# First block on one core: token rows transposed before their norm is known, the norm applied to the projections instead

## The chip, the cores and the metric

The kernel runs on one core of a Trainium2 chip, as one program. The metric is the device time of that core in microseconds (us), from several runs of the same program; a smaller number is better. TensorE does the matrix products, ScalarE and VectorE do everything elementwise, GpSimd some small steps, and SyncE issues nearly all transfers from HBM.

## The reference, cut to what matters

Two transformer blocks over 256 tokens of width 1024. The part that the change touches is the start of the first block:

```
h = rms_norm(x, norm_mix)                 # x * rsqrt(mean(x*x) + eps) * gain
z = h @ w_in                              # (256, 2560)
zu, zv, zq, zk, zval = split(z)           # 512 columns each
u = gelu(zu);  v = gelu(zv)
a_out = u * (tril(W_s) @ layer_norm(v) + b)
o = differential_attention(q = zq / 8, k = zk, v = zval)
x = x + concat(a_out, norm(o)) @ w_out
x = x + memory_attention(rms_norm(x), rms_norm(mem), w_q_mem, w_kv_mem, w_o_mem)
x = x + mixture_of_32_experts(rms_norm(x))
```

A second block (attention and a squared-ReLU feed-forward of width 4096) and a last norm follow. All of it is fp32.

## The kernel before, in words

The 256 tokens are two halves of 128 rows (h = 0 and 1). A weight matrix is taken in units of 1 MB, each of which is split into a rounded high part, which ScalarE makes (`high(u)`, line 494, 128x2048), and a low part, the rest, which VectorE makes (`low(u)`, line 523, 128x2048). A product is then three matmuls, lines 433, 434 and 435 (`three`). The order of units in the first block is v.0, v.1, u0, u1, q0, k0, val.0, val.1, q1, k1, km0, km1, km2, out0 and so on. The first two are split in four pieces each (`rows_high`, line 891, and `rows_lows`, line 1112). Units share two sets of high and low tiles in turn, so `high(u)` of a unit waits until TensorE has ended the unit two places before.

The orders in which the engines work are written out by hand, one list per engine (`first_tensor`, `first_scalar`, `first_vector`, `first_sync`, `first_gpsimd`). Each engine takes its own list strictly in order and waits on semaphores of the others.

Before the change the rows of x are normed first. ScalarE squares and sums each half (`square_sum`, line 511), VectorE adds the epsilon (line 540), GpSimd takes the power -1/2 (line 548), and ScalarE and VectorE each scale half of the columns (lines 515 and 542). Then TensorE transposes the scaled rows (`turn`, line 484) into the PSUM banks hT00, hT01, hT10 and hT11 (half of the tokens, half of the features), and ScalarE and VectorE make the high part (`turned_highs`, line 505) and the low part (`turned_lows`, line 532) of the transposed rows, with the gain. The 256 rows of the memory go the same way later (memT); TensorE transposes them between the units u0 and u1.

Products leave their banks so: v.0 and v.1 (tokens in rows) through a Gelu on ScalarE; u0 and u1 (features in rows, tokens in columns) through a Gelu on ScalarE; q0, k0, q1 and k1 through a copy on ScalarE (`feature_out`, line 497); val.0 and val.1 through a copy on VectorE. The attention over pairs (head, half of the queries) goes by `diff_scores`, `diff_soft_a`, `diff_exp`, `diff_soft_b`, `diff_turn`, `diff_apply` for u = 0 to 7. `diff_scores(0)` waits for q0 and k0 to have left their banks, `diff_scores(4)` for q1 and k1. `gating` (lines 707 and 708) makes the product with W_s and adds the bias.

TensorE's list around the change, in short: transpose x; v.0; v.1; u0; transpose mem; u1; q0; transpose W_s; k0; diff_scores(0); val.0; diff_scores(1); gating; val.1; diff_scores(2); diff_turn(0); q1; diff_scores(3); diff_turn(1); diff_apply(0); k1; diff_scores(4); diff_turn(2); diff_apply(1); km0; and on.

Of the kernel before, what the change touches and what calls it, by code (L numbers as in the profile page):

```python
# [9 lines left out]
ALU = mybir.AluOpType  # L10
# [120 lines left out]
hT00 hT01 hT10 hT11 +v.0 +v.1 -v.0 -v.1 u0@2 memT00@6 memT01@7 memT10@0 memT11@1 u1@3 q0@4 sguw@5 k0@2 +O0@6 +O1@7  # L131
# [26 lines left out]
def build_program(nc, a, out):  # L158
# [148 lines left out]
    rows_v = Count(nc, "scaled_rows_v", ("h0", "h1", "mem0", "mem1", "xq0", "xq1", "p0", "p1"))  # L307
    rows_s = Count(nc, "scaled_rows_s", ("h0", "h1", "mem0", "mem1", "xq0", "xq1", "ffn0", "ffn1", "x0", "x1"))
    turned = Count(nc, "turned", [f"{t}{h}{c}" for t in ("hT", "memT") for h in range(2) for c in range(2)]
                   + ["sguw", "oT0", "oT1"]  # L310
                   + [f"{t}{h}{c}" for t in ("xqT", "fT", "pT", "eT") for h in range(2) for c in range(2)] + ["r2"])
    norm_wide = Count(nc, "norm_wide", ("f0", "f1"))
    t_high = Count(nc, "turned_high", [f"hT{h}{c}" for c in range(2) for h in range(2)]
                   + [f"{t}{h}{c}" for t in ("memT", "xqT", "pT", "eT") for h in range(2)
# [11 lines left out]
    masked = Count(nc, "sgu_masked", ("sguw",))  # L326
    gate_mm = Count(nc, "sgu_multiplied", (0, 1))
# [41 lines left out]
    gated = [t.rearrange("p (g t) -> p g t", g=GROUPS) for t in (arena[5][:, 1536:2048], arena[6][:, 1024:1536])]  # L369
    memX, kmT = tok(ring[:, 2 * PIECE:2 * PIECE + UNIT]), chunks(arena[3])  # L370
# [127 lines left out]

    def turned_highs(plan, tag, h, dst, gain, count_tag=None, groups=(0, 1)):
# [63 lines left out]
    def first_sync():  # L563
        for h in range(NH):
            SP.dma_start(X[:, h, :], a["x"][0, h * P:(h + 1) * P, :]).then_inc(*loads.inc(f"x{h}"))
        for u in order1[0:2]:
            load_first(u)
        for h in range(NH):
            SP.dma_start(memX[:, h, :], a["mem"][0, h * P:(h + 1) * P, :]).then_inc(*loads.inc(f"mem{h}"))
        for u in order1[2:4]:  # L570
            load_first(u)
# [76 lines left out]
    def first_tensor():  # L648
# [117 lines left out]
        turn(bank1, "hT", [(rows_v.at(f"h{h}"), rows_s.at(f"h{h}")) for h in range(NH)])  # L766
# [114 lines left out]
    def first_scalar():  # L881
        def high(u):
            round_high(u, order1, lanes1, lane1_sem, parts1, buffer1, high1, unit1)

        def rows_high(u):
            n = order1.index(u)
            SC.wait_ge(lane1_sem[n], 16)
            for c in range(4):
                o = slice(512 * c, 512 * (c + 1))
                done = row_high.inc(f"{u}{c}") if c < 3 else high1.inc(u)  # L890
                SC.activation(parts1[buffer1[0][u]][0][:, o], lanes1[n][:, o], ACT.Copy).then_inc(*done)
# [74 lines left out]
        SC.wait_ge(*loads.after("gain_mem", 1))  # L966
        turned_highs(bank1, "memT", 0, memT[0], G_MEM)
        turned_highs(bank1, "memT", 1, memT[0], G_MEM)
        feature_out("u1", flat(uT[:, 2:4, :]), func=ACT.Gelu)
        high("k0")  # L970
        feature_out("q0", flat(qT[:, 0:2, :]), float(DQK) ** -0.5)
# [5 lines left out]
        feature_out("k0", flat(kT[:, 0:2, :]))  # L977
# [10 lines left out]
        feature_out("q1", flat(qT[:, 2:4, :]), float(DQK) ** -0.5)  # L988
# [3 lines left out]
        feature_out("k1", flat(kT[:, 2:4, :]))  # L992
# [109 lines left out]
    def first_vector():  # L1102
        def low(u):
            take_low(u, order1, lanes1, parts1, buffer1, high1, split1)

        def rows_lows(u):
# [137 lines left out]
        low("val.0")  # L1244
# [18 lines left out]
        DVE.wait_ge(*bank1.freed("u0"))  # L1263
        DVE.wait_ge(*bank1.freed("u1"))
# [1151 lines left out]
```

## Time and profile before

| | |
|---|---|
| median of 3 runs | 1017.67 us (1015.38 to 1018.61) |
| the profiled execution, its own time | 1017.38 us |
| span of that execution | 1016.1 us |
| TensorE matmul busy | 963.8 us, 95% of the span |
| VectorE busy | 441.9 us, 43% |
| ScalarE busy | 358.7 us, 35% |
| GpSimd busy | 26.2 us, 3% |
| first block up to the experts | about the first 245 us |
| experts | about 245 to 704 us |
| second block | from about 704 us |

Times in the rows are counted from the start of the span. PE is TensorE, PEld its weight loads, ACT ScalarE, DVE VectorE, POOL GpSimd, SP SyncE. In a row of the timeline the first number is the start, the second the duration, and a bracket at the end names the idle time ahead of the instruction and what released it. PEclk is the granted clock of TensorE; 1.00 is the full level, 0.50 the half.

### The profile page before, as it was taken

How to read it: one execution, taken by the hardware profiler on the slowest of the kernel's cores; microseconds unless marked ns; L12 is line 12 of the kernel's file. 1: busy time of each engine (PE TensorE's matmuls, PEld its weight loads, DVE VectorE, ACT ScalarE, POOL GpSimd, SP SyncE). 2: the span in 40 equal slices, each digit the busy share in tenths (PEclk: the TensorE clock that was granted, in tenths of full speed). 3: DMA queues.
4: the chain of work that ended last, by engine and by line, in shares of the span. 5: the costliest groups of instructions: out<-in, count | busy, mean ns of one | idle time of the engine just before them, and what ended most of it. 6: DMA issues, size and time to landing. Idle time of an engine off the chain costs nothing.

```text
span 1016.1 us, 13622 instructions
## 1 busy us (share of the span) xinstructions
PE 963.8 (95%) x5353; PEld 647.1 (64%) x5353; DVE 441.9 (43%) x757; ACT 358.7 (35%) x593; POOL 26.2 (3%) x40
## 2 busy tenths in 40 slices
PE   6999989998999999999999999996999989999997
PEld 5979878985343443334334334332998879998886
DVE  5756565445222222222213222124664665555434
ACT  7735436442221121121111112114554554554332
POOL 1310000000000000000000000000000000000000
PEclk9989999998999999999999999998999999999999
DMA  9943543486699999999999999999645535555601
GB/s 319 362 143 124 167 136 143 166 309 269 280 429 427 428 428 429 429 428 429 428 429 429 429 428 430 427 430 363 214 160 166 165 104 167 171 195 175 205 1 41
DMA packets 71758, 289.57 MB, mean 285 GB/s; under 512 B 4897, under 2 KB 44449, under 8 KB 59426
## 3 DMA queue, kind: packets, MB, share of 16 engines
q1 hardware_dynamic: 71138, 288.79, 73.4%
q8 instruction: 31, 0.51, 0.2%
q10 hardware_dynamic: 576, 0.17, 0.1%
q14 instruction: 13, 0.11, 0.0%
HBM read 287.90 MB, written 1.05 MB: 284 GB/s over the span
## 4 chain that ended last, share of the span: by engine, by line
PE 82%; ACT 6%; issue 5%; DVE 5%; POOL 1%; DMA 0%; ACTq 0%; SPq 0%; DVEq 0%
PE bank L1520 22%; PE bank L433 11%; PE bank L1542 11%; PE bank L435 11%; PE bank L434 11%; PE bank L1493 5%; PE bank L1553 3%; ACT w_high L494 3%; PE bank L1512 1%; DVE w_low L523 1%; DVE arena L2273 1%; ACT hidden_high L2097 1%; ACT arena L1565 1%; PE bank L723 1%; PE bank L761 1%
## 5 line engine op out<-in xcount | busy, mean ns | idle before, releaser
L1520 PE MATMUL bank<-ring,arena 128*64 128x512 f32 x1024 | 228.8, 599 | 0.3 <-issue 0.3
L523 DVE TENSOR_TENSOR w_low<-ring,w_high 128x2048 fp32r<-128x2048 f32 x76 | 174.1, 2291 | 122.8 <-ACT w_high L494 122.7
L494 ACT ACTIVATE w_high<-ring 128x2048 fp32r<-128x2048 f32 x76 | 145.1, 1909 | 122.9 <-PE bank L435 122.8
L1520 PEld LDWEIGHTS bank<-ring,arena 128*64 128x64 f32 x1024 | 71.1, 137 | 132.6 <-issue 132.4
L1542 PE MATMUL bank<-ring,arena 128*64 128x512 f32 x512 | 116.9, 598 | 1.0 <-issue 1.0
L433 PE MATMUL bank<-xT_high,w_high 128*128 128x256 f32 x384 | 111.5, 290 | 2.6 <-DVE xT_low L532 1.8
L434 PE MATMUL bank<-xT_low,w_high 128*128 128x256 f32 x384 | 109.3, 285 | 0.0
L435 PE MATMUL bank<-xT_high,w_low 128*128 128x256 f32 x384 | 109.2, 284 | 0.0
L1585 ACT ACTIVATE y_high<-bank,arena 64x512 fp32r<-64x512 f32 x64 | 43.7, 683 | 155.3 <-DVE arena L1632 84.0
L1645 DVE SCALAR_TENSOR_TENSOR y_low<-bank,arena,y_high 64x512 fp32r<-64x512 f32 x64 | 48.0, 750 | 85.8 <-ACT y_high L1585 85.4
L433 PEld LDWEIGHTS bank<-xT_high,w_high 128*128 128x128 f32 x384 | 74.2, 193 | 4.4 <-issue 2.0
L1572 ACT ACTIVATE arena<-bank 128x256 f32<-128x256 f32 x32 | 12.3, 385 | 177.6 <-PE bank L1520 177.6
L434 PEld LDWEIGHTS bank<-xT_low,w_high 128*128 128x128 f32 x384 | 74.3, 194 | 0.1
L435 PEld LDWEIGHTS bank<-xT_high,w_low 128*128 128x128 f32 x384 | 74.3, 193 | 0.0
L1542 PEld LDWEIGHTS bank<-ring,arena 128*64 128x64 f32 x512 | 34.3, 136 | 61.6 <-issue 59.6
L1639 DVE TENSOR_TENSOR arena<-bank,arena 128x256 f32<-128x256 f32 x32 | 13.6, 425 | 105.7 <-ACT arena L1572 105.7
L1493 PE MATMUL bank<-onehot,rows_high 128*128 128x192 f32 x176 | 46.0, 297 | 9.1 <-ACT arena L1565 8.1
L1493 PEld LDWEIGHTS bank<-onehot,rows_high 128*128 128x128 f32 x176 | 34.6, 197 | 31.3 <-issue 19.4
L433 PE MATMUL bank<-w_high,hidden_high 128*128 128x512 f32 x128 | 50.0, 390 | 0.7 <-DVE arena L2273 0.6
L434 PE MATMUL bank<-w_low,hidden_high 128*128 128x512 f32 x128 | 49.8, 389 | 0.0
L435 PE MATMUL bank<-w_high,hidden_low 128*128 128x512 f32 x128 | 49.8, 389 | 0.0
L1632 DVE TENSOR_REDUCE arena<-bank 128x1 f32<-128x256 f32 x32 | 13.6, 425 | 78.4 <-PE bank L1512 77.9
(280 smaller groups left out, 1492.5 us busy)
## 6 DMA issues: line engine op xcount, KB each, us to landing
ring<-in_w_gate SPq DMA_DIRECT2D x32, 2048.0 KB, 18.4
ring<-in_w_up SPq DMA_DIRECT2D x32, 2048.0 KB, 22.9
ring<-in_w_down SPq DMA_DIRECT2D x32, 2048.0 KB, 21.9
ring<-in_w_up SPq DMA_DIRECT2D x16, 1024.0 KB, 5.8
ring<-in_w_down SPq DMA_DIRECT2D x16, 1024.0 KB, 4.8
ring<-in_attn_w_qkv SPq DMA_DIRECT2D x12, 1024.0 KB, 12.1
ring<-in_w_in SPq DMA_DIRECT2D x10, 1024.0 KB, 11.8
ring<-in_w_kv_mem SPq DMA_DIRECT2D x8, 1024.0 KB, 5.1
```

Of the source, the lines that this page charges most:

```text
L433: PE.matmul(o, lh, rh, start=start, stop=False, skip_group_check=True)
L434: PE.matmul(o, lh, rl, start=False, stop=False, skip_group_check=True)
L435: return PE.matmul(o, ll, rh, start=False, stop=stop, skip_group_check=True)
L494: SC.activation(parts[buffer[0][u]][0][:, :], lanes[n % len(lanes)], ACT.Copy).then_inc(*high.inc(u))
L523: DVE.tensor_tensor(p[1][:, :], lanes[n % len(lanes)], p[0][:, :].bitcast(F32), ALU.subtract).then_inc(*split.inc(u))
L1493: last = PE.matmul(bank[:, c * width:(c + 1) * width], part[:, h, k * P:(k + 1) * P], ONEHOT[buffer][:, h, 0:width], start=h == 0 and part ...
L1520: last = PE.matmul(GU[t * SLOTS:(t + 1) * SLOTS, 0:NGU], xs[:, k, :], wgu[:, :, k, t * (DE // JT):(t + 1) * (DE // JT)], start=k == 0, sto ...
L1542: last = PE.matmul(DN[t * SLOTS:(t + 1) * SLOTS, 0:NY], HT[:, o:o + SLOTS], wd[:, k, (t ^ odd) * NY:((t ^ odd) + 1) * NY], start=k == 0, s ...
L1553: last = PE.matmul(ACC[2 * h + t][:, :], ROUTET[:, b, t, h, :], y[:, :], start=False, stop=True, skip_group_check=True)
L1585: last = SC.activation(Y[t][0][p, :], DN[p, 0:NY], ACT.Copy, scale=SLOT_WEIGHT[p, b, t:t + 1])
L1632: DVE.tensor_reduce(SLOT_WEIGHT[:, b, o:o + 1], MISC[:, 0:NH * P], AX, ALU.add).then_inc(*q.inc("slot_weight"))
L1645: last = DVE.scalar_tensor_tensor(out=Y[t][1][p, :], in0=DN[p, 0:NY], scalar=SLOT_WEIGHT[p, b, t:t + 1], in1=Y[t][0][p, :].bitcast(F32), o ...
```

## The change

The token rows are transposed raw, as soon as a half of x has landed. The gain still multiplies the transposed rows, but the factor of each token no longer does. The sums of squares come later on ScalarE, after the high part of u0. VectorE spreads the factor of each half over a 128x128 tile (`norm_wide`), TensorE turns the two tiles into a bank rh between u0 and u1, and ScalarE copies that bank to a row tile (128x256, `evacuate_part`). The factor is then applied where the products leave their banks: for v as the scale of the Gelu on ScalarE, for val as the scalar of the copy on VectorE, and for u0, u1, q0, k0, q1 and k1 by a new VectorE instruction (`features_out`, a scalar_tensor_tensor from PSUM with the row tile broadcast). For u0 and u1 a Gelu in place follows on ScalarE (`u_gelus`).

The transposes of mem move behind u1, the load of mem behind that of u0, the high and low parts of memT are made for half 1 first and later, and the banks of some later tiles change. The loads, the matmuls and the split of the weights are the same in number.

```diff
 FIRST_BANKS = """
-hT00 hT01 hT10 hT11 +v.0 +v.1 -v.0 -v.1 u0@2 memT00@6 memT01@7 memT10@0 memT11@1 u1@3 q0@4 sguw@5 k0@2 +O0@6 +O1@7
+hT00 hT01 hT10 hT11 +v.0 +v.1 -v.0 -v.1 u0@2 rh@6 u1@3 memT00@6 memT01@7 memT10@0 memT11@1 q0@4 sguw@5 k0@2 +O0@6 +O1@7
...
     def first_sync():
...
-        for u in order1[0:2]:
+        for u in order1[0:3]:
             load_first(u)
         for h in range(NH):
             SP.dma_start(memX[:, h, :], a["mem"][0, h * P:(h + 1) * P, :]).then_inc(*loads.inc(f"mem{h}"))
-        for u in order1[2:4]:
-            load_first(u)
+        load_first(order1[3])
...
         PE.wait_ge(*consts.at("ident"))
-        turn(bank1, "hT", [(rows_v.at(f"h{h}"), rows_s.at(f"h{h}")) for h in range(NH)])
+        turn(bank1, "hT", [(loads.after(f"x{h}", 1),) for h in range(NH)], src=X)
...
         f("u0", hT)
+        bank = open_bank(bank1, "rh")
+        for h in range(NH):
+            PE.wait_ge(*norm_wide.at(f"h{h}"))
+            last = PE.transpose(bank[:, h * P:(h + 1) * P], wide_h[:, h * P:(h + 1) * P], ident[:, :])
+        last.then_inc(*turned.inc("rh"))
+        f("u1", hT)
         turn(bank1, "memT", [(rows_v.at(f"mem{h}"), rows_s.at(f"mem{h}")) for h in range(NH)], src=memX)
-        f("u1", hT)
         f("q0", hT)
...
+        def u_gelus(u, t):
+            SC.wait_ge(*bank1.freed(u))
+            SC.activation(t, t, ACT.Gelu).then_inc(*u_gelu.inc(u))
...
-        for h in range(NH):
-            SC.wait_ge(*loads.after(f"x{h}", 1))
-            square_sum(X[:, h, :], XN[:, h, :], f"h{h}", stat("h", h))
-        for h in range(NH):
-            scale_half("h", h, XN, X)
         SC.wait_ge(*loads.after("gain_mix", 1))
         turned_highs(bank1, "hT", 0, hT[0], G_MIX, groups=(0,))
+        turned_highs(bank1, "hT", 1, hT[0], G_MIX, groups=(0,))
         rows_high("v.0")
-        turned_highs(bank1, "hT", 1, hT[0], G_MIX, groups=(0,))
         turned_highs(bank1, "hT", 0, hT[0], G_MIX, groups=(1,))
         turned_highs(bank1, "hT", 1, hT[0], G_MIX, groups=(1,))
         rows_high("v.1")
         high("u0")
         for h in range(NH):
+            SC.wait_ge(*loads.after(f"x{h}", 1))
+            square_sum(X[:, h, :], XN[:, h, :], f"h{h}", stat("h", h))
+        for h in range(NH):
             SC.wait_ge(*loads.after(f"mem{h}", 1))
             square_sum(memX[:, h, :], arena[4][:, 1024 * h:1024 * (h + 1)], f"mem{h}", stat("mem", h))
+        high("u1")
         for h in range(NH):
             scale_half("mem", h, memX, memX)
-        SC.wait_ge(*early1.at("v.1"))
-        evacuate(bank1, "v.0", v[:, 0, :], func=ACT.Gelu)
-        SC.wait_ge(*unit1.at("v.1"))
-        evacuate(bank1, "v.1", v[:, 1, :], func=ACT.Gelu)
-        high("u1")
-        feature_out("u0", flat(uT[:, 0:2, :]), func=ACT.Gelu)
+        for h, whole in ((0, early1), (1, unit1)):
+            SC.wait_ge(*whole.at("v.1"))
+            SC.wait_ge(*rstd.at(f"h{h}"))
+            evacuate(bank1, f"v.{h}", v[:, h, :], stat("h", h), ACT.Gelu)
         high("q0")
+        SC.wait_ge(*turned.at("rh"))
+        evacuate_part(bank1, "rh", row_h)
+        u_gelus("u0", flat(uT[:, 0:2, :]))
+        high("k0")
+        u_gelus("u1", flat(uT[:, 2:4, :]))
         SC.wait_ge(*loads.after("gain_mem", 1))
+        turned_highs(bank1, "memT", 1, memT[0], G_MEM)
         turned_highs(bank1, "memT", 0, memT[0], G_MEM)
...
-        feature_out("k0", flat(kT[:, 0:2, :]))
         high("val.1")
...
         high("k1")
-        feature_out("q1", flat(qT[:, 2:4, :]), float(DQK) ** -0.5)
...
         high("km0")
-        feature_out("k1", flat(kT[:, 2:4, :]))
...
+        def features_out(u, dst, scale):
+
+            DVE.wait_ge(*unit1.at(u))
+            DVE.wait_ge(*bank1.freed("rh"))
+            DVE.scalar_tensor_tensor(out=dst, in0=banks[bank1.bank[u]][:, :].rearrange("p (n t) -> p n t", t=S),
+                                     scalar=scale, in1=row_h.rearrange("p (n t) -> p n t", n=1).to_broadcast([P, 2, S]),
+                                     op0=ALU.mult, op1=ALU.mult).then_inc(*bank1.inc(u))
...
         low("u0")
+        for h in range(NH):
+            r = stat("h", h)
+            DVE.wait_ge(*squares.at(f"h{h}"))
+            DVE.tensor_scalar(r, r, RMS_EPS, None, ALU.add).then_inc(*meansq.inc(f"h{h}"))
+        for h in range(NH):
+            DVE.wait_ge(*rstd.at(f"h{h}"))
+            DVE.tensor_scalar(wide_h[:, h * P:(h + 1) * P], ones[:, :], stat("h", h), None,
+                              ALU.mult).then_inc(*norm_wide.inc(f"h{h}"))
         for h in range(NH):
             DVE.wait_ge(*loads.after(f"mem{h}", 1))
             mean_and_scale("mem", h, memX, memX)
         low("u1")
+        features_out("u0", uT[:, 0:2, :], 1.0)
...
         low("q0")
-        turned_lows(bank1, "memT", 0, memT, G_MEM)
+        features_out("u1", uT[:, 2:4, :], 1.0)
+        low("k0")
         turned_lows(bank1, "memT", 1, memT, G_MEM)
-        low("k0")
...
+        features_out("q0", qT[:, 0:2, :], float(DQK) ** -0.5)
+        low("val.0")
+        features_out("k0", kT[:, 0:2, :], 1.0)
         DVE.wait_ge(*lam_exp.at("exp"))
         DVE.tensor_tensor(lam[:, 0:1], lam[:, 3:4], lam[:, 2:3], ALU.subtract).then_inc(*lam_done.inc("minus"))
+        turned_lows(bank1, "memT", 0, memT, G_MEM)
...
         diff_soft_a(2)
         diff_soft_b(2)
+        features_out("q1", qT[:, 2:4, :], float(DQK) ** -0.5)
         low("k1")
         diff_soft_a(3)
         diff_soft_b(3)
+        features_out("k1", kT[:, 2:4, :], 1.0)
         low("km0")
```

## Rows read from the trace of the kernel before

**Rows 1.** The page: TensorE's busy time, and the chain that ended last, by engine.

```profile
PE 963.8 (95%) x5353; PEld 647.1 (64%) x5353; DVE 441.9 (43%) x757; ACT 358.7 (35%) x593; POOL 26.2 (3%) x40
...
PE 82%; ACT 6%; issue 5%; DVE 5%; POOL 1%; DMA 0%; ACTq 0%; SPq 0%; DVEq 0%
```

**Rows 2.** Windows, expert stage: us, then busy times, PEclk, DMA share, GB/s.

```profile
300.00:400.00 100.00, 97.78 (x480) 40.15 (x478) 26.19 (x56) 18.16 (x38) 0.00 (x0) 1.00 1.01 428
```

**Rows 3.** The chain that ended last, 0 to 14 us: start, us, what.

```profile
1.27 4.67 DMA arena<-in_x
...
7.87 1.10 PE bank L484 x4
9.06 1.15 ACT hT_high L505 x4
10.23 1.13 DVE hT_low L532 x4
11.36 0.61 DVE w_low L1112
...
12.11 0.76 PE bank L433
```

**Rows 4.** Windows, the first 7.8 us.

```profile
0.00:7.80 7.80, 0.00 (x0) 0.00 (x0) 0.76 (x3) 4.39 (x7) 2.69 (x13) 1.00 0.72 269
```

**Rows 5.** ScalarE's timeline, 0 to 31 us.

```profile
4.68 1.06 ACT L511 ACTIVATE arena<-arena 128x1024 f32<-128x1024 f32 x1 [1.91 <-DMA arena<-in_x]
...
10.08 2.20 ACT L891 ACTIVATE w_high<-ring 128x512 fp32r<-128x512 f32 x4
...
20.10 1.92 ACT L494 ACTIVATE w_high<-ring 128x2048 fp32r<-128x2048 f32 x1 [2.65 <-PE bank L435]
...
27.03 1.28 ACT L497 ACT_TABLE_LOAD   x1
28.32 1.08 ACT L497 ACTIVATE arena<-bank 128x512 f32<-128x512 f32 x2
```

**Rows 6.** VectorE's timeline, 31 to 36 us.

```profile
31.24 2.29 DVE L523 TENSOR_TENSOR w_low<-ring,w_high 128x2048 fp32r<-128x2048 f32 x1 [4.47 <-ACT w_high L494]
33.45 1.64 DVE L1228 BATCH_NORM_STATS2 arena<-arena 128x6 f32<-128x128 f32 x8
```

**Rows 7.** TensorE's timeline, the transposes of mem and the start of u1.

```profile
31.04 1.91 PE L484 MATMUL bank<-ident,ring 128*128 128x128 f32 x16
33.59 0.38 PE L433 MATMUL bank<-hT_high,w_high 128*128 128x256 f32 x1 [0.64 <-DVE w_low L523]
```

**Rows 8.** Groups by line and form, 0 to 150 us: busy us, mean ns.

```profile
L1296 DVE SCALAR_TENSOR_TENSOR mixed_low<-bank,small,mixed_high 128x512 fp32r<-128x512 f32 x2 | 1.4, 744 | 0.0
...
L911 ACT ACTIVATE arena<-bank 128x256 f32<-128x256 f32 x4 | 1.5, 386 | 5.4 <-PE bank L684 5.4
```

**Rows 9.** ScalarE's and TensorE's timelines around 52 us.

```profile
51.61 1.07 ACT L497 ACTIVATE arena<-bank 128x512 f32<-128x512 f32 x2
...
52.78 0.49 PE L675 MATMUL bank<-arena 64*128 64x128 f32 x4 [1.24 <-issue]
```

**Rows 10.** VectorE's and TensorE's timelines, 79 to 91 us.

```profile
79.57 2.29 DVE L523 TENSOR_TENSOR w_low<-ring,w_high 128x2048 fp32r<-128x2048 f32 x1 [0.87 <-ACT w_high L494]
...
81.33 0.70 PE L675 MATMUL bank<-arena 64*128 64x256 f32 x4
...
82.38 0.36 PE L433 MATMUL bank<-hT_high,w_high 128*128 128x256 f32 x1
...
89.25 0.49 PE L675 MATMUL bank<-arena 64*128 64x128 f32 x4 [0.88 <-ACT arena L497]
...
90.21 0.36 PE L433 MATMUL bank<-memT_high,w_high 128*128 128x256 f32 x1
```

**Rows 11.** Windows, the clock's fall near 64 us and an idle stretch near 132.

```profile
64.40:67.40 3.00, 3.00 (x11) 2.02 (x9) 2.30 (x2) 0.06 (x1) 0.00 (x0) 0.54 0.00 0
67.40:71.50 4.10, 4.10 (x10) 3.23 (x11) 2.67 (x4) 1.26 (x2) 0.00 (x0) 0.51 0.68 256
...
129.00:136.00 7.00, 4.25 (x30) 3.56 (x29) 5.84 (x7) 3.67 (x4) 1.02 (x1) 1.00 0.15 43
```

More of the change, by code:

```diff
@@ L306, in build_program @@
                               "z1", "a0", "a1", "pre0", "pre1", "y0", "y1"))
-    rows_v = Count(nc, "scaled_rows_v", ("h0", "h1", "mem0", "mem1", "xq0", "xq1", "p0", "p1"))
-    rows_s = Count(nc, "scaled_rows_s", ("h0", "h1", "mem0", "mem1", "xq0", "xq1", "ffn0", "ffn1", "x0", "x1"))
-    turned = Count(nc, "turned", [f"{t}{h}{c}" for t in ("hT", "memT") for h in range(2) for c in range(2)]
+    rows_v = Count(nc, "scaled_rows_v", ("mem0", "mem1", "xq0", "xq1", "p0", "p1"))
+    rows_s = Count(nc, "scaled_rows_s", ("mem0", "mem1", "xq0", "xq1", "ffn0", "ffn1", "x0", "x1"))
+    turned = Count(nc, "turned", [f"hT{h}{c}" for h in range(2) for c in range(2)] + ["rh"]
+                   + [f"memT{h}{c}" for h in range(2) for c in range(2)]
                    + ["sguw", "oT0", "oT1"]
                    + [f"{t}{h}{c}" for t in ("xqT", "fT", "pT", "eT") for h in range(2) for c in range(2)] + ["r2"])
-    norm_wide = Count(nc, "norm_wide", ("f0", "f1"))
+    norm_wide = Count(nc, "norm_wide", ("h0", "h1", "f0", "f1"))
     t_high = Count(nc, "turned_high", [f"hT{h}{c}" for c in range(2) for h in range(2)]
-                   + [f"{t}{h}{c}" for t in ("memT", "xqT", "pT", "eT") for h in range(2)
+                   + [f"memT{h}{c}" for h in (1, 0) for c in range(2)]
+                   + [f"{t}{h}{c}" for t in ("xqT", "pT", "eT") for h in range(2)
                                        for c in range(2)])
@@ L326, in build_program @@
     masked = Count(nc, "sgu_masked", ("sguw",))
+    u_gelu = Count(nc, "u_gelu", ("u0", "u1"))
     gate_mm = Count(nc, "sgu_multiplied", (0, 1))
@@ L369, in build_program @@
     gated = [t.rearrange("p (g t) -> p g t", g=GROUPS) for t in (arena[5][:, 1536:2048], arena[6][:, 1024:1536])]
+    wide_h, row_h = arena[1][:, 0:S], arena[6][:, 2048 - S:2048]
     memX, kmT = tok(ring[:, 2 * PIECE:2 * PIECE + UNIT]), chunks(arena[3])
@@ L497, in evacuate, with evacuate_part @@
         SC.activation(dst, banks[plan.bank[name]][:, :], func or ACT.Copy, scale=scale).then_inc(*plan.inc(name))
+    def evacuate_part(plan, name, dst):
+        SC.activation(dst, banks[plan.bank[name]][:, 0:dst.shape[1]], ACT.Copy).then_inc(*plan.inc(name))
     def turned_highs(plan, tag, h, dst, gain, count_tag=None, groups=(0, 1)):
@@ L954, in first_scalar @@
         for h in range(NH):
+            SC.wait_ge(*loads.after(f"x{h}", 1))
+            square_sum(X[:, h, :], XN[:, h, :], f"h{h}", stat("h", h))
+        for h in range(NH):
             SC.wait_ge(*loads.after(f"mem{h}", 1))
             square_sum(memX[:, h, :], arena[4][:, 1024 * h:1024 * (h + 1)], f"mem{h}", stat("mem", h))
+        high("u1")
         for h in range(NH):
             scale_half("mem", h, memX, memX)
-        SC.wait_ge(*early1.at("v.1"))
-        evacuate(bank1, "v.0", v[:, 0, :], func=ACT.Gelu)
-        SC.wait_ge(*unit1.at("v.1"))
-        evacuate(bank1, "v.1", v[:, 1, :], func=ACT.Gelu)
-        high("u1")
-        feature_out("u0", flat(uT[:, 0:2, :]), func=ACT.Gelu)
-        high("q0")
+        for h, whole in ((0, early1), (1, unit1)):
+            SC.wait_ge(*whole.at("v.1"))
+            SC.wait_ge(*rstd.at(f"h{h}"))
+            evacuate(bank1, f"v.{h}", v[:, h, :], stat("h", h), ACT.Gelu)
+        high("q0")
+        SC.wait_ge(*turned.at("rh"))
[3 more added lines that the diff above has]
+        u_gelus("u1", flat(uT[:, 2:4, :]))
         SC.wait_ge(*loads.after("gain_mem", 1))
+        turned_highs(bank1, "memT", 1, memT[0], G_MEM)
         turned_highs(bank1, "memT", 0, memT[0], G_MEM)
[L968 to L971, printed above, removed]
         high("val.0")
@@ L1211, in first_vector @@
         for h in range(NH):
-            DVE.wait_ge(*loads.after(f"x{h}", 1))
-            mean_and_scale("h", h, XN, X)
-        turned_lows(bank1, "hT", 0, hT, G_MIX, groups=(0,))
+            turned_lows(bank1, "hT", h, hT, G_MIX, groups=(0,))
         rows_lows("v.0")
-        turned_lows(bank1, "hT", 1, hT, G_MIX, groups=(0,))
-        turned_lows(bank1, "hT", 0, hT, G_MIX, groups=(1,))
-        turned_lows(bank1, "hT", 1, hT, G_MIX, groups=(1,))
+        for h in range(NH):
+            turned_lows(bank1, "hT", h, hT, G_MIX, groups=(1,))
         rows_lows("v.1")
         low("u0")
+        for h in range(NH):
+            r = stat("h", h)
+            DVE.wait_ge(*squares.at(f"h{h}"))
+            DVE.tensor_scalar(r, r, RMS_EPS, None, ALU.add).then_inc(*meansq.inc(f"h{h}"))
+        for h in range(NH):
+            DVE.wait_ge(*rstd.at(f"h{h}"))
+            DVE.tensor_scalar(wide_h[:, h * P:(h + 1) * P], ones[:, :], stat("h", h), None,
+                              ALU.mult).then_inc(*norm_wide.inc(f"h{h}"))
         for h in range(NH):
@@ L1243, in first_vector @@
             last.then_inc(*vnorm.inc(n))
-        low("val.0")
         DVE.wait_ge(*loads.after("lambda", 5))
@@ L1262, in first_vector @@
         DVE.wait_ge(*bank1.freed("sguw"))
-        DVE.wait_ge(*bank1.freed("u0"))
-        DVE.wait_ge(*bank1.freed("u1"))
+        DVE.wait_ge(*u_gelu.at("u1"))
         for n in range(NH):
@@ L1273, in first_vector @@
             DVE.wait_ge(*(early1 if h == 0 else unit1).at("val.1"))
-            DVE.tensor_scalar(vv[:, h, :], banks[bank1.bank[f"val.{h}"]][:, :], 1.0, None,
+            DVE.tensor_scalar(vv[:, h, :], banks[bank1.bank[f"val.{h}"]][:, :], stat("h", h), None,
                               ALU.mult).then_inc(*bank1.inc(f"val.{h}"))
```

## The prediction

> **What bounds the kernel now.** I read the page first. TensorE is busy 95% of the span and is 82% of the chain that ended last; DMA is 0% of it [rows 1]. So a change to the first 100 us counts only by how much later or earlier it lets TensorE's list run. The windows of the expert stage come next: 97.8 of 100 us busy on TensorE, with the DMA engines full at 428 GB/s [rows 2]. That looks like a second bound, but the chain there names matmuls and no transfer, and each new expert load is released by a matmul, so the loads shift with TensorE. I carry a shift at 100 us to the end at one to one.
>
> The chain of the first 14 us shows what the change goes at. The second half of x lands at 5.94; then come its squares, the scaling, the first transposes (7.87), the first high part (9.06), its low part (10.23), the first weight piece's low part (11.36), and the first matmul of v.0 at 12.11 [rows 3]. From there to the transposes of mem at 31.04, TensorE runs without a gap (v.0, v.1, u0), then waits 0.64 us for u1's low part [rows 7].
>
> I work in shifts of TensorE's list against before: a negative one is earlier.
>
> **The start.** x half 0 has landed at 4.68, where ScalarE's wait for it ends [rows 5]. Transposes come at 1.10 us for the first four, some 0.9 for each four after. So hT00 is in its bank at 5.8, and hT10, the third group, at 7.6. The high part of four chunks takes 1.15, the low part 1.13 [rows 3]. ScalarE: hT00 from 5.8, hT10 from 7.6 to 8.75, then v.0's first piece (2.20/4, so with its start-up about 0.65 [rows 5]) to 9.4. VectorE: hT10's low part 8.75 to 9.9, then the first piece's low part 0.61 to 10.6 [rows 3]. First matmul at 10.6 + 0.14 = 10.75, a shift of -1.36. What could take this is v.0 itself: 269 GB/s over 7.8 us is 2.1 MB [rows 4], just x and v.0, so its last byte moves at 7.8, and with the delay to its semaphore it is there by about 8.7. The other bound is 10.08, where before ScalarE took it up without waiting [rows 5]; that would make the shift zero.
>
> **To u1.** v.1, u0 keep the shift: v.1's first low part is ready near 15.2, wanted at 18.5. Removing the norm chain is thus worth 1.36 here, not the 3.2 by which the transposes move, as v.0's split and the second half's chunks now stand in the way. The transposes of mem (1.91) leave the place between u0 and u1, two for rh take it (2/16 of 1.91, 0.24), and the 0.64 wait can go [rows 7]. ScalarE: high u0 at 20.10 - 1.36 = 18.74 [rows 5], to 20.6; four squares (1.06 each, 2.1 a pair) to 24.8; high u1 to 26.65. The squares of x, 2.1, cost TensorE nothing, since u0's 5.75 us of matmuls cover them. The load of mem, now behind u0's, comes one 1 MB load later, 2.6 us at the rate of [rows 4] and above, by about 17, and is wanted at 22.7. VectorE: the factors, the two wide tiles and the mem rows end at 27.1, low u1 (2.29 [rows 6]) at 29.4. TensorE ends u0 at 29.68 and rh at 29.9: no wait, by half a us.
>
> **To q0.** Here the new waits begin. ScalarE after high u1: mem's halves to 27.9, the table load 1.28 and two Gelus 1.08 [rows 5] to 30.3, high q0 to 32.2, the copy of rh (0.39 [rows 8]) to 32.55. VectorE stands at features_out(u0) from 29.4 until then, with everything for q0 queued behind. I price this instruction by the nearest row, a scalar_tensor_tensor from PSUM of 128x512: 0.74 [rows 8]; nothing else in the trace has its broadcast operand, and 0.69 to 1.4 bounds it. Then the statistics of v, 1.64 [rows 6] and 0.64 and 0.17 from the same timeline, from 33.4, low q0 from 35.8 to 38.05. TensorE ends u1 at 35.7 and mem's transposes at 37.6, so it waits 0.5. q0 starts at 38.1 against 39.36 (33.59 + 48 matmuls at 0.12): shift -1.25.
>
> The Trainium skill, page ScalarE: Activation LUTs, section What ACT_TABLE_LOAD costs, gives a drain of about 1.38 us with each table load. Here the load ends at 28.31 and the Gelu starts at 28.32 [rows 5], so no drain shows; by the page q0 would start about 1.4 later and the shift be gone, by the row it stays. I go by the row.
>
> **To gating.** VectorE after low q0: features_out(u1), low k0, memT's half 1, the centring of v (4.3), the lambda sums, features_out(q0), low val.0 to 51.0, features_out(k0) to 51.75. q0 and k0 now leave on VectorE; before, k0's copy ended at 52.68 and diff_scores(0) started at 52.78 [rows 9]. Now it starts at 51.85: shift -0.93. low val.1 ends near 57.0 and is wanted at 66.4, so memT's half 0, moved ahead of it, costs nothing; if that cover of 9 us were gone it would be 2.1. Gating's own inputs (GpSimd's gain and mask, by 53.5) are ready before 58.6.
>
> **Where it is given back.** After diff_soft_b(2), VectorE's list now has features_out(q1) ahead of low k1. It waits for the end of q1, and low k1 is queued behind it. Before, low k1 ran at 79.57 to 81.86, under q1's matmuls, and k1 started 1.05 us after q1's end (81.33 to 82.38), with diff_scores(3), diff_turn(1) and diff_apply(0) between [rows 10]. Now: q1 ends at 81.33 - 0.93 = 80.4, +0.1 for the semaphore, +0.74, +2.29, +0.05: k1 starts at 83.55 or a little less, as start-ups overlap by 0.1. So the gap of 1.05 becomes 3.1, and the shift goes from -0.93 to +1.1.
>
> The same again for k1: features_out(k1) stands ahead of low km0. Before, km0 started 90.21 - 88.29 = 1.9 after k1's end, with a wait of 0.88 for k1's copy in it [rows 10]. Now it is again 3.1, 1.2 more: shift +2.3. After km0 the order has no further evacuation on VectorE ahead of a split; low km1 is ready at 98.7, wanted at 99.5. The shift stays at +2.3.
>
> Sum against the profiled execution: -1.36 (start) + 0.11 (q0) + 0.32 (diff_scores(0)) + 2.05 (k1) + 1.2 (km0) = +2.3 us. Its time was 1017.38, 1.3 above its span, and 0.3 under the median of the runs. 1017.38 + 2.3 is 1019.7, and from the median 1020.0; I take 1019.8, +0.2%.
>
> **The clock.** TensorE falls to half its clock near 64.4 and is back at 71.5 [rows 11], that is 1.2 GHz in place of 2.4, while it was busy with gating, costing about 3.5 us. In the 7 us from 129, TensorE was idle for 2.75 and kept the full clock [rows 11]. The new gaps (3.1 with 1 us of small work in each) are like that one. The Trainium skill, page TensorE: Matmul & The Clock Gate, Part 1, has the clock fall after idleness; the fall at 64.4 came without any, so the trace does not follow it there. Its own result would be a fall at the new gaps, the third rival.
>
> **The rivals.**
> - The gain holds and the waits are covered (faster side). This needs low k1 not to be stuck behind features_out(q1). The bare sum is then -0.93 or, were the start to follow the transposes fully, -3.2. Against it: VectorE's list is strict and the gap before was 1.05 for 3.1 us of work. It decides for faster only if both stalls are gone and the start gives 3.1. With a change of clock phase of 2 more it could be 1013. Chance 0.05 for over 0.3% faster.
> - The start gives nothing, v.0 landing at 10: then +1.36 more, 1021.1. Chance 0.15.
> - One more stretch at half clock, at the gaps at 81 or 91, of the price of that at 64: +3.5, 1023.3. Chance 0.12.
> - The stretch near 64 to 71 is missed, or the clock rises earlier at the start: -3.5 to -1, 1016.3 to 1018.8. Chance 0.15.
> - As worked out, 1019.8, give or take 1: the rest, 0.53.
>
> **Chances.** The runs of before spread by 3.2 us; a change of 0.3%, 3.05 us, is about what can be told from none. Faster than 1014.6 is 0.05. Slower than 1020.7 takes in the third rival, most of the second and a fifth of the main case: 0.3. The rest, 0.65, is no change. The range from 1016.8 to 1022.8 leaves out about 2 in 10.
>
> **What would show it.** In the profile after: the first matmul of v.0 near 10.8; q0's start near 38.1 with a wait for low q0; VectorE idle near 29.5 to 32.6 waiting for ScalarE's copy of rh; features_out near 0.74 each; diff_scores(0) near 51.9; TensorE idle about 2 us ahead of k1 and 1.2 ahead of km0, both released by a low part on line 523's successor; the expert stage with the same length. I am wrong if low k1 runs under q1's matmuls, if the first matmul is at 12, or if features_out costs over 1 us, which adds its excess twice at the two stalls.

## The result, and the profile after

The changed kernel takes 1021.61 us (median of 6 runs, 1021.22 to 1022.25), the kernel before 1017.88 beside it (6 runs, 1015.38 to 1018.61). The ratio is 1.0043, with a 95% interval of 1.0032 to 1.0055: slower by 0.43%, or 4.4 us, more than the 0.3% that the prediction counts as the least that can be told from nothing. The profiled execution after took 1021.9 us, and its span of 1020.5 is 4.4 us longer than that of before.

First the page of the kernel after, its busy times and its chain's sources, which answer to [rows 1]. Then the chain of its first 12 us, which answers to [rows 3].

```profile
PE 966.8 (95%) x5355; PEld 649.8 (64%) x5355; DVE 444.7 (44%) x763; ACT 355.3 (35%) x588; POOL 25.9 (3%) x40
```

```profile
0.82 3.64 DMA arena<-in_x
...
4.59 2.81 PE bank L488 x12
...
7.42 1.15 ACT hT_high L512 x4
...
8.60 1.12 DVE hT_low L539 x4
9.72 0.61 DVE w_low L1131
...
10.46 0.47 PE bank L437
```

The norm chain is gone from the start. The first matmul of v.0 comes at 10.46, against 12.11 in [rows 3]. The busy sums hardly move: the loss is not work.

Next the timeline of TensorE of the kernel after, the instructions that waited or stand between the units.

```profile
10.46 0.47 PE L437 MATMUL bank<-w_high,hT_high 128*128 128x512 f32 x1 [2.57 <-DVE w_low L1131]
...
28.80 0.38 PE L783 MATMUL bank<-ident,arena 128*128 128x128 f32 x2
...
37.10 0.39 PE L437 MATMUL bank<-hT_high,w_high 128*128 128x256 f32 x1 [0.41 <-DVE w_low L530]
...
50.36 0.49 PE L681 MATMUL bank<-arena 64*128 64x128 f32 x4 [1.05 <-issue]
...
78.87 0.70 PE L681 MATMUL bank<-arena 64*128 64x256 f32 x4
...
81.92 0.39 PE L437 MATMUL bank<-hT_high,w_high 128*128 128x256 f32 x1 [1.75 <-DVE w_low L530]
90.40 0.49 PE L681 MATMUL bank<-arena 64*128 64x128 f32 x4 [0.98 <-DVE arena L1121]
...
92.40 0.39 PE L437 MATMUL bank<-memT_high,w_high 128*128 128x256 f32 x1 [0.81 <-DVE w_low L530]
```

And VectorE's timeline of the kernel after where the two evacuations stand ahead of the low parts (line 1121 is `features_out`, line 530 the low part).

```profile
31.73 0.69 DVE L1121 SCALAR_TENSOR_TENSOR arena<-bank,arena 128x512 f32<-128x512 f32 x1 [3.46 <-ACT arena L504]
...
78.98 0.69 DVE L1121 SCALAR_TENSOR_TENSOR arena<-bank,arena 128x512 f32<-128x512 f32 x1 [2.67 <-PE bank L439]
79.58 2.28 DVE L530 TENSOR_TENSOR w_low<-ring,w_high 128x2048 fp32r<-128x2048 f32 x1
...
89.46 0.69 DVE L1121 SCALAR_TENSOR_TENSOR arena<-bank,arena 128x512 f32<-128x512 f32 x1 [3.64 <-PE bank L439]
90.06 2.28 DVE L530 TENSOR_TENSOR w_low<-ring,w_high 128x2048 fp32r<-128x2048 f32 x1
```

TensorE's timeline of the kernel before, where its q0 starts, 48 matmuls behind the start of u1 in [rows 7] (the prediction put it at 39.36):

```profile
39.44 0.28 PE L433 MATMUL bank<-hT_high,w_high 128*128 128x256 f32 x1
```

The bracket of the row at 78.98 shows VectorE idle for 2.67 us until TensorE ended q1; low k1 could only then begin, and the row of TensorE at 81.92 shows 1.75 us idle for it. So each landmark stands against before, in us (before from [rows 3, 9, 10] and the line above):

| landmark on TensorE's list | before | after | shift | forecast shift |
|---|---|---|---|---|
| first matmul of v.0 | 12.11 | 10.46 | -1.65 | -1.36 |
| q0 starts | 39.44 | 37.10 | -2.34 | -1.25 |
| diff_scores(0) | 52.78 | 50.36 | -2.42 | -0.93 |
| diff_scores(3), behind q1 | 81.33 | 78.87 | -2.46 | -0.93 |
| k1 starts | 82.38 | 81.92 | -0.46 | +1.1 |
| diff_scores(4), behind k1 | 89.25 | 90.40 | +1.15 | +1.1 |
| km0 starts | 90.21 | 92.40 | +2.19 | +2.3 |
| end of the span | 1016.1 | 1020.5 | +4.4 | +2.3 |

The shift goes from -2.46 to +4.4, and the two stalls explain 3.1 of these 6.9 us. Windows of the kernel after show most of the rest. Columns as in [rows 2]: us, busy times, then PEclk, DMA share, GB/s.

```profile
10.40:14.80 4.40, 4.34 (x12) 3.46 (x13) 4.40 (x13) 4.40 (x13) 0.00 (x0) 0.61 1.08 367
62.00:68.60 6.60, 6.60 (x19) 4.86 (x18) 4.54 (x6) 2.11 (x3) 0.00 (x0) 0.50 0.35 106
82.20:85.60 3.40, 3.40 (x19) 3.40 (x19) 2.03 (x6) 2.05 (x5) 0.00 (x0) 0.54 0.78 251
92.80:96.10 3.30, 3.30 (x17) 3.30 (x17) 1.45 (x5) 2.60 (x5) 0.00 (x0) 0.50 0.70 236
```

TensorE ran at about half its clock (1.2 GHz of 2.4) right behind each of the two stalls. With a granted clock of 0.54 over 3.4 us and 0.50 over 3.3, that is 3.4 x 0.46 = 1.6 and 3.3 x 0.50 = 1.65 us of matmul time. Before had neither stretch. The stretch in gating is there in both ([rows 11] has before's). From km1 on the shift is +3.7, at the experts +3.9 (their loads are issued at 265.02 against 261.13, and near their end at 656.08 against 652.20), and +4.4 behind them. The carry at one to one held through the DMA-heavy stage. The last 0.5 arises at one wait of TensorE near the end of that stage, here in the kernel before and after:

```profile
685.91 7.09 PE L1520 MATMUL bank<-ring,arena 128*64 128x512 f32 x32 [0.33 <-issue]
```

```profile
690.25 7.09 PE L1549 MATMUL bank<-ring,arena 128*64 128x512 f32 x32 [0.80 <-issue]
```

The profile names nothing that ends this wait. It lasts from 0.33 to 1.01 us in the twelve profiles of this case, so its half microsecond can't be put down to the change.

### The profile page after: what moved, and what is told of

Its sections match the earlier page's. It is cut to its first block, busy times and chain, and to the rows that moved or that the text cites. A ratio compares the mean times of both kernels' runs of the same rounds, so it can differ in the third digit from the quotient of the medians.

```text
span 1020.5 us, 13631 instructions
## 1 busy us (share of the span) xinstructions
PE 966.8 (95%) x5355; PEld 649.8 (64%) x5355; DVE 444.7 (44%) x763; ACT 355.3 (35%) x588; POOL 25.9 (3%) x40
## 3 DMA queue, kind: packets, MB, share of 16 engines
HBM read 287.90 MB, written 1.05 MB: 283 GB/s over the span
## 4 chain that ended last, share of the span: by engine, by line
PE 81%; ACT 7%; DVE 5%; issue 5%; POOL 0%; DMA 0%; ACTq 0%; DVEq 0%
PE bank L1549 22%; PE bank L1571 11%; PE bank L437 11%; PE bank L438 11%; PE bank L439 11%; PE bank L1522 5%; PE bank L1582 3%; ACT w_high L498 3%; DVE w_low L530 1%; PE bank L1541 1%; DVE arena L2302 1%; ACT hidden_high L2126 1%; PE bank L488 1%; ACT arena L1594 1%; PE bank L729 1%
```

## The experiments

The ratios that follow are to the kernel before, run beside it on the same chip. The runs of before alone spread from 1015.0 to 1019.1.

**Both evacuations behind the low parts.** In VectorE's list of the kernel after:

```diff
-        features_out("q1", qT[:, 2:4, :], float(DQK) ** -0.5)
         low("k1")
+        features_out("q1", qT[:, 2:4, :], float(DQK) ** -0.5)
         diff_soft_a(3)
         diff_soft_b(3)
-        features_out("k1", kT[:, 2:4, :], 1.0)
         low("km0")
+        features_out("k1", kT[:, 2:4, :], 1.0)
```

> The kernel after, with the evacuation of q1 put behind low k1 and that of k1 behind low km0 on VectorE. Theory A (the order makes two stalls of 2.0 and 1.1 us, and each stall brings a stretch of half clock worth 1.5 us): all 6.1 us come back, TensorE's list is about 2.4 us ahead of before from q1 on, the time is 2.4 us under before, near 1015.5. Rival B (only the stalls themselves belong to the order, the half clock comes by chance in any version): 3.1 us come back, 1018.5. Rival C (VectorE is too full with the evacuations wherever they stand, so the waits move to diff_scores(4) or to a later low part): less than 2 us come back, over 1019.5.

Measured: 1018.39 us, ratio 1.0007 (0.9998 to 1.0016). 3.2 us came back of the kernel after's 1021.61, which in number is what Rival B said, and theory A's 1015.5 is missed. The profile shows why it is not simply Rival B. TensorE's and VectorE's timelines of this kernel:

```profile
87.87 0.49 PE L681 MATMUL bank<-arena 64*128 64x128 f32 x4 [1.93 <-DVE arena L1121]
```

```profile
84.72 2.29 DVE L530 TENSOR_TENSOR w_low<-ring,w_high 128x2048 fp32r<-128x2048 f32 x1 [0.67 <-ACT w_high L498]
86.93 0.68 DVE L1121 SCALAR_TENSOR_TENSOR arena<-bank,arena 128x512 f32<-128x512 f32 x1
```

The stall ahead of k1 is gone. But k1 now ended at 85.9, low km0 was in work until 86.93, and the evacuation had to wait for it. The wait ahead of diff_scores(4) became 1.93 us, where the kernel after had 0.98 there and 0.81 ahead of km0, 1.79 together. So the place of k1's evacuation behind low km0 gains nothing; both orders put 2.3 us of split and 0.7 of evacuation in a gap that has room for one. That the wait moves to diff_scores(4) is what Rival C had said, though with a time over 1019.5. And behind that gap of 1.93 the clock fell again, from 89 to 93.

**Each alone.** Only one of the two swaps.

> The kernel after, with only the evacuation of q1 put behind low k1; that of k1 stays ahead of low km0. Theory A: 2.0 for the stall and 1.5 for the half clock behind it come back, 1018.1, with one stretch of half clock left after km0's start. Rival B: 2.0 come back, 1019.6. Rival C: within 1 us of the kernel after, 1021.

> The kernel after, with only the evacuation of k1 put behind low km0; that of q1 stays ahead of low k1. Theory A: 1.1 for the stall and 1.5 for the half clock behind it come back, 1019.0, with one stretch of half clock left after k1's start. Rival B: 1.1 come back, 1020.5. Rival C: within 1 us of the kernel after, 1021.

Measured: q1 behind alone 1018.69 us, ratio 1.0012 (1.0003 to 1.0022); k1 behind alone 1020.26, ratio 1.0026 (1.0017 to 1.0035). The q1 swap gives 2.9 back of the kernel after's 1021.61, between theory A's 3.5 and Rival B's 2.0. The k1 swap gives 1.3 back, near Rival B's 1.1, and its interval just overlaps that of the kernel after (1.0032 to 1.0055). Both together give no more than q1's alone (the intervals of 1018.39 and 1018.69 overlap). The order of q1 is the change's one large fault. In the profile of the q1 swap, waits of 0.98 and 0.80 stand around diff_scores(4) as in the kernel after, and this time no fall of the clock follows them. In that of the k1 swap, the wait of 1.76 ahead of k1 is there, and no fall follows it either:

```profile
82.00:86.00 4.00, 4.00 (x34) 4.00 (x35) 2.44 (x7) 2.45 (x5) 0.00 (x0) 1.00 0.69 243
```

The half clock comes there from 90 to 94, behind a wait of 1.69 ahead of diff_scores(4). So theory A's "each stall brings a stretch" is too strong.

**The part of the loss alone, in the kernel before.** The copies of q1 and k1 on VectorE, ahead of the low parts:

```diff
+            DVE.wait_ge(*unit1.at(u))
+            DVE.tensor_scalar(dst, banks[bank1.bank[u]][:, :], scale, None, ALU.mult).then_inc(*bank1.inc(u))
...
         diff_soft_b(2)
+        copy_out("q1", flat(qT[:, 2:4, :]), float(DQK) ** -0.5)
         low("k1")
         diff_soft_a(3)
         diff_soft_b(3)
+        copy_out("k1", flat(kT[:, 2:4, :]), 1.0)
         low("km0")
```

> The kernel before, with one part of the change alone: the copies of q1 and k1 out of their banks go to VectorE, and stand ahead of low k1 and low km0. Theory A (this order is what costs): k1 starts 2.0 us and km0 another 1.1 us later, so at least 3.1 over before, 1020.6, and up to 1.5 more for each stretch of half clock that a gap brings, at most 1023.7. Rival D (the loss lies in the banks, in rh or in the later memory rows): within 1 us of before, 1017.5.

Measured: 1023.5 us, ratio 1.0054 (1.0035 to 1.0073), which is 6.2 over before by the medians and 5.5 by the ratio, at the upper end of theory A. Rival D is out. TensorE's timeline of this kernel has the same stalls as the kernel after, at the same sizes:

```profile
84.19 0.39 PE L433 MATMUL bank<-hT_high,w_high 128*128 128x256 f32 x1 [1.76 <-DVE w_low L523]
92.68 0.49 PE L675 MATMUL bank<-arena 64*128 64x128 f32 x4 [0.98 <-DVE arena L1106]
94.68 0.39 PE L433 MATMUL bank<-memT_high,w_high 128*128 128x256 f32 x1 [0.80 <-DVE w_low L523]
```

Its windows of one microsecond show the half clock from 84 to 89 and from 95 to 99, again one stretch behind each stall. With 3.1 for the stalls, 3.1 of the 6.2 are left, about what two such stretches cost in the kernel after (1.6 and 1.65). In the profiles, the distance to before grows from -0.2 us at diff_scores(3) (81.14 against 81.33) to 6.0 at diff_scores(5) (102.13 against 96.13).

**The gaps filled.** The kernel after, with matmuls that TensorE does while it would wait. Their result goes to the bank of k1 (km0), where the first real matmul overwrites it:

```diff
         diff_apply(0)
+        fill("k1", 14)
         f("k1", hT)
...
             diff_apply(u - 3)
+            if u == 4:
+                fill("km0", 6)
             f(f"km{u - 4}", memT)
```

> The kernel after, with 14 matmuls of 128x256 whose result is overwritten put on TensorE ahead of k1 and 6 ahead of km0, so that it works through both waits; the waits themselves stay. Theory A (the half clock is brought by the idle gaps): the two stretches at half clock go, 3.0 us come back, 1018.6, while k1 and km0 start as late after the evacuations as before. Rival B (the half clock does not hang on the gaps): 1021.6 or a little more.

Measured: 1019.27 us, ratio 1.0025 (1.0015 to 1.0035). That is 2.3 under the kernel after (3.0 was expected, and none by Rival B), with k1 and km0 still held until their low parts are ready. Three of its ten runs lie at 1021.1 to 1021.5, as long as those of the kernel after. Windows of this kernel, then of the kernel after:

```profile
82.00:86.00 4.00, 3.93 (x32) 3.93 (x33) 2.60 (x8) 2.30 (x5) 0.00 (x0) 1.00 0.74 242
...
92.00:97.00 5.00, 5.00 (x43) 4.88 (x41) 3.11 (x5) 2.68 (x5) 0.00 (x0) 1.00 0.64 210
```

```profile
82.00:86.00 4.00, 4.00 (x21) 4.00 (x22) 2.44 (x7) 2.45 (x5) 0.00 (x0) 0.57 0.76 254
...
92.00:97.00 5.00, 4.60 (x26) 4.60 (x27) 2.98 (x9) 2.68 (x5) 0.00 (x0) 0.66 0.60 210
```

The clock is 1.00 where it was 0.57 and 0.66. One profile would not be enough for this, since the clock stayed up behind two unfilled gaps in the swaps above. All twelve profiles together are. Between 77 and 100 us they hold ten places where TensorE idles for 1.7 to 1.9 us, in one piece or as 0.98 and 0.8 close together, and the clock falls behind eight of them. Nowhere else in that stretch does it fall, neither at the start of k1 in the nine profiles without a wait there nor behind a single wait of up to 0.98. The half clock hangs on the idle gaps, not on the units, but it does not follow each of them.

**The squares of x back at the start.** The first experiment, with `square_sum` of x ahead of the first high part on ScalarE instead of behind high u0.

> The first experiment (both evacuations behind) with the squares of x put back ahead of the first high part on ScalarE; the transposes still take raw rows. By the rows after, hT00's high part then starts at 7.0 in place of 5.8 and the first matmul comes near 11.3, 0.85 us later; the wait of 0.4 ahead of q0 goes in return, as ScalarE has 2.1 us less behind u0. So +0.4 against the first experiment, 1018.8. Rival: the squares cost all of their 2.3 us at the start, 1020.7.

Measured: 1018.95 us, ratio 1.0024 (1.0012 to 1.0036). The median is near the expected 1018.8. The first matmul is at 11.02 against 10.47 (0.85 later was expected), and the wait ahead of q0 is gone. The difference to the first experiment is 0.56 us by the medians and 1.7 by the ratios, whose intervals overlap, so these runs can't tell it. The profile can't price the squares either: q0 starts at 38.49 there against 37.09, but 1.3 of these 1.4 us are a longer half clock in v.0, and a shorter one in gating gives them back (diff_scores(3) at 78.81 against 78.90).

**low km0 taken out of the way.** The kernel after with the evacuation of q1 behind low k1, and:

```diff
+        high("km0")
         diff_exp(3)
-        high("km0")
...
         diff_soft_a(3)
+        low("km0")
         diff_soft_b(3)
         features_out("k1", kT[:, 2:4, :], 1.0)
-        low("km0")
```

> The kernel after with the evacuation of q1 behind low k1, and with high km0 ahead of diff_exp(3) on ScalarE and low km0 ahead of diff_soft_b(3) on VectorE, so that neither low part waits for an evacuation and k1's evacuation follows k1 at once. Theory A: the wait ahead of diff_scores(4) is 1.0 in place of 1.9, TensorE's list is 2.3 us ahead of before at km0, and the clock's fall near 89 loses its gap: 1.0 to 2.5 us under the first experiment, 1015.9 to 1017.4. Rival E (falls of the clock come as often with short gaps): 1017.4 or more.

Measured: 1016.03 us, ratio 0.9991 (0.9982 to 1.0000), 2.4 under the first experiment by the medians and 1.6 by the ratios. VectorE's and TensorE's timelines of this kernel:

```profile
82.67 2.29 DVE L530 TENSOR_TENSOR w_low<-ring,w_high 128x2048 fp32r<-128x2048 f32 x1 [0.47 <-ACT w_high L498]
...
86.43 0.69 DVE L1121 SCALAR_TENSOR_TENSOR arena<-bank,arena 128x512 f32<-128x512 f32 x1 [0.42 <-PE bank L439]
```

```profile
87.37 0.49 PE L681 MATMUL bank<-arena 64*128 64x128 f32 x4 [0.98 <-DVE arena L1121]
```

Low km0 is done at 84.96, the evacuation follows k1 at once, and the wait is 0.98. The clock stays at 1.00 from 77 to 97. The time is in theory A's range (1015.9 to 1017.4), and Rival E does not show. Against the kernel before, the gain is not told from none. Of the 2.9 us between the spans of this profile and of the first experiment's (1014.7 and 1017.6), part is a stretch at half clock from 133 to 141 that only the latter has, where the two kernels have the same work.

**The same with a warm start.** TensorE transposes the identity, 12 times ahead of x's transposes and 10 times behind them:

```diff
+        warm(12)
         turn(bank1, "hT", [(loads.after(f"x{h}", 1),) for h in range(NH)], src=X)
+        warm(10)
```

> The previous kernel with 12 transposes of the identity, overwritten later, on TensorE ahead of the transposes of x and 10 behind them, so that it has no idle stretch from 1.7 us on. If the half clock of the first 4.5 us of v.0 comes from the idle start, TensorE enters v.0 at 2.4 GHz and the list gains up to 2.2 us: 1014 to 1015. If the rival holds, that the start's half clock does not hang on what TensorE did before, nothing changes or the extra work delays the first matmul by some tenths.

Measured: 1014.94 us, ratio 0.9982 (0.9970 to 0.9994): faster than both kernels by its median, by 0.18% than before, an amount under the 0.3% though its interval excludes 1. Its interval overlaps that of the kernel without the warm start. TensorE's timeline of this kernel shows the start at the full clock, since matmuls of 512 columns are 0.23 to 0.24 apart from the second on, where the chain of the kernel before has 0.43 from 12.9 to 16.3 us:

```profile
7.17 1.25 PE L774 MATMUL bank<-ident 128*128 128x128 f32 x10
9.98 0.47 PE L437 MATMUL bank<-w_high,hT_high 128*128 128x512 f32 x1 [1.56 <-DVE w_low L1138]
10.29 0.40 PE L438 MATMUL bank<-w_low,hT_high 128*128 128x512 f32 x1
10.53 0.40 PE L439 MATMUL bank<-w_high,hT_low 128*128 128x512 f32 x1
```

q0 starts at 35.05, 2.45 before the previous kernel's 37.50. The medians differ by 1.1 only. In the profile the lead is gone at the first expert load (174.60 against 174.32), behind a fall of the clock from 129 to 136 that the previous kernel's lacks. By 259 us it is 1.3 ahead again (258.09 against 259.43), as a stretch at half clock near 245 is shorter, and both spans are 1014.7. So the start gained 2.5 us on the list, and later stretches at half clock decide what is left of it. A start at the full clock does not need the warming either: the profile with k1's evacuation alone behind has it too.

**The memory rows in their old place.** The first experiment with mem's transposes behind u0 again and rh behind them in v.1's bank:

```diff
-... u0@2 rh@6 u1@3 memT00@6 memT01@7 memT10@0 memT11@1 q0@4
+... u0@2 memT00@6 memT01@7 memT10@0 memT11@1 rh@5 u1@3 q0@4
```

> The first experiment (both evacuations behind) with the transposes of mem back in their old place behind u0, and rh behind them in the bank of v.1. By the theory the later memory rows cost and bring next to nothing: u1 starts 1.9 us later, q0 at the same time or up to 0.4 us earlier, as its wait for low q0 is then covered; 1018.0 to 1018.6. Rival: the place of mem is part of what the change brings, and u1's delay pushes low k0 and diff_scores(0) later by 1 us or more, over 1019.4.

Measured: 1023.86 us (4 runs, 1020.26 to 1024.59), ratio 1.0067 (1.0045 to 1.0090). The theory missed, and the rival is right. q0 started at 36.94, as expected, 0.15 earlier. But u1 ended 1.9 us later, high k0 waits for that end, low k0 came at 38.54 in place of 37.56, and all that VectorE does behind it came a microsecond later: diff_scores(0) at 51.37 against 50.35, with a wait of 2.23 against 1.05. The half clock in gating then lasted from 61 to 72, against 62 to 69, and diff_scores(4) came at 90.30 against 87.87, 2.4 later. That shift stays through the experts (656.10 against 653.68 for one of their last loads), and the span is 4.2 longer, so 1.8 arise behind them. The one microsecond on the list is shown, and the other 1.4 us up to diff_scores(4) go with the longer half clock in gating. Of the 1.8, 0.6 are the wait near the end of the experts (1.01 against 0.43). Why the rest of the 5.5 between the medians came out is open, and 4 runs are few.

**A warm start in the kernel before.** 34 transposes of the identity ahead of the transposes of x.

> The kernel before with 34 transposes of the identity on TensorE ahead of the transposes of x, in its idle time from 1.6 to 7.9 us; nothing else is changed. If the warm start alone explains what the best kernel gained by it, v.0 runs at 2.4 GHz from 12.1 on, up to 2.2 us come off, near 1015.2 to 1016.3, and the best kernel with the change is then about 1 us faster than this one. Rival: the half clock at the start returns with v.0's own waits, no gain, 1017.4.

Measured: 1016.55 us, ratio 1.0006 (0.9995 to 1.0017), beside runs of before with a median of 1015.77. No gain can be told. The profiled execution does have its list 2.5 us ahead (diff_scores(4) at 86.79 against 89.25) and took 1015.48. What takes the gain back in the others, the profile of one execution can't show. So the warm start alone does not explain the best kernel.

## Why the prediction was right, and where it was off

The direction, the place and the price of the two stalls were right. The time lies in the range (1021.6 in 1016.8 to 1022.8), but 1.8 above the point, and on the slower side of 0.3% to which I gave 0.3 against 0.65 for no change. That it lies in the range is in part luck. Two steps missed in opposite ways: up to q1's end the list gained 1.5 us more than forecast, and the clock took 3.25 that were not forecast. With the start as forecast the time would have been near 1023.1, outside the range. By its own steps:

- **The start.** Forecast -1.36, measured -1.65: transposes at 0.9 for four were 0.8, and the prediction's own rows add up to 10.65, not 10.75 (9.9 + 0.61 + 0.14). v.0 had landed, as ScalarE took it up at 8.48 without waiting, so the second rival is out.
- **To q0 and diff_scores(0).** Forecast -1.25 and -0.93, measured -2.34 and -2.42. The order of waits was right: VectorE idle for 3.46 until rh was copied, then a wait of 0.41 for low q0 (forecast 0.5). Two sizes were off. The first matmul of v.0 still ran at the full clock, and the half clock behind it lasted 3.4 us (matmuls 0.43 apart from 10.9 to 14.3) where before had 4.6 from its first matmul on; so v.0 ended 2.2 earlier (high u0 starts at 17.87 against 20.10 in [rows 5]), not 1.36. And low val.0 ended at 49.66, forecast 51.0, so features_out(k0) could start just behind k0's end. The load of mem, priced at 2.6 us, is 3.9 at the 269 GB/s of [rows 4], but nothing waited for it. A table load of 1.28 us is there again (26.99), and the Gelu starts at 28.28, as [rows 5] had it. The Trainium skill, page ScalarE: Activation LUTs, section What ACT_TABLE_LOAD costs, has 1.38 us of drain more; the trace does not agree.
- **How firm the start's gain is.** The kernel after and five of the experiments (both behind, each alone, gaps filled, low km0 taken out of the way) do the same work in the same order up to q1's end, yet TensorE's q0 starts anywhere from 35.50 to 38.55 in their profiles. The two ends are the swaps of k1 alone and of q1 alone:

```profile
35.50 0.38 PE L437 MATMUL bank<-hT_high,w_high 128*128 128x256 f32 x1 [0.43 <-DVE w_low L530]
```

```profile
38.55 0.39 PE L437 MATMUL bank<-hT_high,w_high 128*128 128x256 f32 x1 [0.44 <-DVE w_low L530]
```

  The half clock in v.0 makes most of the difference: its matmuls lose nothing to it in the first and 2.7 us in the second, 1.55 in the kernel after and 2.3 in that of before. The half clock in gating then evens part of it out. At q1's end the six lie 0.9 to 2.5 us ahead of before, five of them about 2.0 or more. The forecast -0.93 is within this spread.
- **features_out.** 0.69 each, taken at 0.74.
- **The stall ahead of k1.** Forecast 2.05, measured -0.46 + 2.46 = 2.00. The experiment in the kernel before gave the same idle time, 1.76 against 1.75.
- **The stall ahead of km0.** Forecast 1.2, measured 2.19 - 1.15 + 0.10 = 1.14, with the 0.1 by which the wait ahead of diff_scores(4) grew (0.98 against 0.88). Here my reading that it comes from the evacuation standing ahead of the low part was incomplete: behind it, it costs as much (1.93 against 1.79). Only low km0 out of the gap takes it away.
- **The clock: the step that failed.** I took it that the gaps keep the full clock, since "the new gaps (3.1 with 1 us of small work in each) are like that one", the idle stretch near 132 in [rows 11]. One execution's row was no evidence of a rule: with the same idle time there, the clock fell at just that place in five of the twelve profiles (both behind, q1 alone behind, gaps filled, warm start with low km0 out of the way, memory rows in the old place). Both new gaps brought a stretch at half clock, worth 1.6 and 1.65. My third rival had one such stretch at 3.5, with a chance of 0.12, priced by the stretch in gating, which is twice as long. The Trainium skill, page TensorE: Matmul & The Clock Gate, Part 1, has the clock fall after idleness, though it does not say that gaps as short as these bring a fall; the filled gaps and the ten places above bear the rule out here, and the result came out nearer to it than to my row. The fall within gating is in all eleven other profiles as in [rows 11], for 3.4 to 10.2 us. No idle stretch is at hand; ahead of it TensorE alternates matmuls of 128 rows and of one row (lines 707 and 708). No run varied these, and its cause is open.

The sum as measured, with shifts on TensorE's list: -2.46 up to q1's end, +2.00 for k1, +1.6 clock, +1.1 for km0, +1.65 clock, makes 3.9, and 3.7 is read from km1's start on. The last 0.5 is the wait near the end of the experts.

Had I priced each gap with the eight falls in ten that the twelve profiles show, 2.6 us more, the point would have been 1022.4, clearly slower. What the change meant to bring is there on TensorE's list (0.9 to 2.5 us at q1's end), but it is hard to show as time: with q1's evacuation and km0's high and low parts moved too, the median is 1.3 us under before, and the interval reaches 1.0000. Only with the extra transposes does it stay below 1.

## What to carry to other kernels

In a kernel like this one, an evacuation that moves to the engine which also splits the next weights belongs behind the split in that engine's strict list, and the following split belongs out of the gap too; count what the gap between two units holds on that engine, before and after. A gap of 1.7 to 1.9 us on TensorE can cost twice: once as idle time, and once as 3.3 us at half clock behind it, which is 1.6 us of work. Compare several profiles before taking one row as proof that a gap is harmless, or one landmark as the gain of a change: with the same list, q0's start moved by 3 us between profiles here.

## What the runs showed that was not expected

- The half clock does not come each time. Behind the same wait of 1.75 us ahead of k1 it fell in the kernel after and in the copies-ahead experiment, but not with k1 alone behind. Behind 0.98 and 0.8 it fell in the same two, and not with q1 alone behind. Behind 1.7 to 1.9 ahead of diff_scores(4) it fell in all four profiles that have it. Behind 0.88 to 0.98 alone it fell in none of the five that have that.
- Twenty-two extra transposes cost nothing, and by the medians the kernel with them is the faster one (1014.94 against 1016.03, with overlapping intervals). They filled idle time.
- The runs of the kernel before bunch near 1015.5 and near 1017.9, on one chip with few between (two of 29 from 1016.0 to 1017.2); on another, seven of 33 lie at 1016.6 to 1017.0. Its profiled execution took 1017.38. The best kernel's runs spread as widely (1013.7 to 1018.0). What separates them was not found. The twelve profiles hold from 31 to 41 us at half clock by the granted clock, and stretches near 133, 250 and 700 to 835 us differ between kernels that do the same work there, so the clock is a candidate.
